# State scan of a delta-rule layer: where one visit of the modulation's products and its transposes stand

## The chip, the cores and the metric

The kernel runs on one core of one Trainium2 chip. The metric is the device time of one execution in microseconds (us). The engines are named as in the profile: PE is TensorE (matmuls), PEld its weight loads, DVE is VectorE, ACT is ScalarE, POOL is GpSimd, SP is SyncE (here the queue that issues the DMAs). The granted clock is the share of TensorE's full speed that the chip allowed.

## The reference, cut to what matters

Two networks run one after the other on 256 tokens of 1024 features. In the first, layers 0 and 3 of four mix their tokens with a delta rule; each head (16 heads of 64) keeps a 64x64 state that is carried over the tokens:

```
def step(state, inp):
    r_t, w_t, k_t, v_t, kk_t, a_t = inp
    sa = jnp.einsum('bhvk,bhk->bhv', state, kk_t)
    state = (state * w_t[:, :, None, :]
             - sa[..., None] * (kk_t * a_t)[:, :, None, :]
             + v_t[..., None] * k_t[:, :, None, :])
    return state, jnp.einsum('bhvk,bhk->bhv', state, r_t)
_, y = lax.scan(step, s0, ...)
```

The second network's two layers are modulated by a vector that depends on the conditions alone, so it can be computed at any earlier time:

```
mx = jnp.split(sc @ w_ada[l] + b_ada[l], N_MOD, axis=-1)
mc = jnp.split(scc @ w_ada[l] + b_ada[l], N_MOD, axis=-1)
```

`w_ada[l]` is a 1024 x 9216 fp32 matrix. Of it the two products have one column each, so what it costs is mostly the reading of the matrix.

## The kernel before, in words

The program is written out by hand for each engine, with semaphores between them; an engine does its instructions in the written order. All matmuls outside the two scans take weights that ACT and POOL split into a high and a low part first.

**The scan** (`pe_scan`, `dve_scan` and the loop over `ch` in `act_rwkv`) runs twice, for layer 0 (from 144.47 us of the profiled execution) and layer 3 (from 1422.81 us). It takes four chunks of 64 tokens (`ch`). In each chunk the recurrence becomes dense algebra on 16 heads, of which half 0 is heads 0 to 7 and half 1 heads 8 to 15 (`HALF`, `halves`):

1. Gram products of the chunk's tokens (lines 1577 and 1582), masked by DVE; for chunks after the first also a product with the carried state (L1611).
2. The right-hand side (L1627), copied by ACT (L1432).
3. The inverse of a triangular 64x64 matrix of each head, by doubling, in levels `lv` 1 to 5. A level has on PE: the first product of half 0 and of half 1 (L1639), each of which ACT copies (L1439); then the second products of half 0 and of half 1 (L1647, and L1650 below level 5), each of which DVE subtracts (L1777, L1780) and masks for the next level (L1746). The first product of a half waits for DVE's work on that half of the level before (`inv_taken`), the second for ACT's copy of that half (`inv_half_taken`).
4. The solution of half 0 and half 1 (L1658), copied by ACT (L1451).
5. Products of outputs and new state that don't need the solution (L1666 and L1669, then L1675), then those that do: outputs L1682 and state L1685, half 0 and half 1, each of which ends with `chunk_out`. ACT copies the outputs (L1454), DVE takes the state (L1807).

**The modulation's products** are put between these. `sp_direct` loads `w_ada` in rounds of four panels of 512 KB each into three sets of buffers; from round 3 on a load waits until the round three before it has been used (`direct_used`). Two rounds of a layer's 18 are used ahead of the scan, four in each chunk. A round is used in two halves (`pe_ada_half`, L1496: four 128x512 matmuls, each of which stands twice in the profile), all in bank 7. In a chunk, `fill()` is called 25 times (`VISITS`); the calls counted in `ADA_VISITS` do one half-round each, eight in all. Visit 0 stands before the right-hand side, visits 4(lv-1)+1 to 4(lv-1)+4 before the four half products of level lv, 21 and 22 before the solution's halves, 23 and 24 before the last products' halves.

After the last half-round of a chunk ACT copies bank 7 to a buffer (`act_ada_rows`, L1511), PE transposes it back (`pe_ada_turn`, L1506, at visit 21) and ACT stores four pieces of it (`act_ada_place`, L1518) as its last work of the chunk. The next chunk's visit 0 waits for that (`ada_ready`), and so does PE after the last chunk.

When the rounds of `w_ada` are issued, SP issues the four first panels of `rw{layer}.out` into the buffers of round 15, as each of those has been used (line 605); ACT converts the first of them after the scan (L633).

Of the kernel before, what the change touches and what calls it, by code (L numbers as in the profile page):

```python
# [221 lines left out]
def build(nc, a, out, CONST_AT):  # L222
# [8 lines left out]
    with ExitStack() as ctx:  # L231
# [766 lines left out]
        def tiles_of(name):  # L998

            return G[name].t0 + G[name].n_tiles  # L1000
# [172 lines left out]
        INV_BANKS = [(bank[0], bank[1], bank[2]), (bank[3], bank[4], bank[6])]  # L1173
        OUT_BANKS, STATE_BANKS = (bank[5], bank[4]), (bank[2], bank[6])
        ADA_BANK = bank[7]
        VISITS = 1 + 5 * 4 + 4
        ADA_VISITS = (0, 3, 6, 9, 12, 15, 18, 20)
        CENTRE = sb("CENTRE", P, at=a_at)
        CENTRED, SPREAD = bank[0:4], bank[4:8]
        FIRST_TILES = 3  # L1180
# [204 lines left out]
        def act_rwkv(act, layer):  # L1385
            j = layer // 3
            parts = lora_parts(layer)
            act_entry(act, layer)
            if layer == 0:
                act_cond(act)  # L1390
            act_lora(act, parts[0], j)
            act_panels(act, f"rw{layer}.k")
            act_lora(act, parts[1], j)
            if layer:
                act_lora(act, parts[2], j)
            act.wait_ge(bank_free, tiles_of(f"rw{layer}.k"))
            act.wait_ge(lora_in, after(act, lora_in, len(parts)))
            for c in range(C):
                cs, scale = slice(c * S, (c + 1) * S), vec("rw_k_k", j, c)
                act.activation(RW_P[:, cs], RW_K[:, cs], ACT.Copy, scale=scale)  # L1400
                op = act.activation(RW_B[:, cs], RW_K[:, cs], ACT.Square, scale=scale)
            op.then_inc(keys_ready, 1)
            tile = act_panels(act, f"rw{layer}.v", by_hand=True)
            tile(0)
            act_lora_mid(act, parts[-1])
            tile(1)
            act.wait_ge(lora_taken, after(act, lora_taken, 8 * len(parts)) - 8)
            for c in range(C):
                cs = slice(c * S, (c + 1) * S)
                op = act.activation(RW_T[:, cs], RW_A[:, cs], ACT.Identity, scale=vec("rw_k_a", j, c), bias=KEPT[:, c:c + 1])  # L1410
            op.then_inc(blend_ready, 1)
            tile(2)
            tile(3)
            act.wait_ge(head_taken, after(act, head_taken))
            act_inverse_root(act, RW_T[:, :])
            act.wait_ge(decay_ready, after(act, decay_ready))
            act.activation(RW_XB[:, :], RW_CUM[:, :], ACT.Exp, scale=DECAY).then_inc(exp_ready, 1)
            act.wait_ge(exp_ready, after(act, exp_ready))
            act.activation(RW_CUM[:, :], RW_CUM[:, :], ACT.Exp, scale=-DECAY).then_inc(exp_ready, 1)
            act.wait_ge(exp_ready, after(act, exp_ready))  # L1420
            for s in range(4, C):
                tile(s)
            act_ada_rows(act, bank[0], ADA_FIRST)
            act_lora_out(act, parts[-1], j)
            act_ada_place(act, layer // 3, bank[0], 0, ADA_FIRST)
            for ch in range(NCH):
                for t, b in ((VT, 1), (BT, 1), (CT, 0)):
                    if ch < NCH - 1 or t is VT:
                        act.wait_ge(turned_ready, after(act, turned_ready))
                        act.activation(t, bank[b][:, :], ACT.Copy).then_inc(turned_taken, 1)  # L1430
                act.wait_ge(rhs_ready, after(act, rhs_ready))
                act.activation(RHS, bank[5][:, :], ACT.Copy).then_inc(rhs_taken, 1)  # L1432
                for lv in range(1, 6):
                    for h, banks in zip(HALF, INV_BANKS):
                        act.wait_ge(inv_half, after(act, inv_half))
                        o, i = IT[:, h], banks[0][:, h]
                        if lv == 5:
                            o, i = blocks(o, lv, 1), blocks(i, lv, 1)
                        act.activation(o, i, ACT.Copy).then_inc(inv_half_taken, 1)  # L1439
                    if ch == 1 and lv < 5:  # L1440
                        if lv == 1:
                            act.wait_ge(bonus_gated, after(act, bonus_gated))
                        for c in (2 * lv - 2, 2 * lv - 1):
                            cs = slice(c * S, (c + 1) * S)
                            op = act.activation(RW_G[:, cs], RW_G[:, cs], ACT.Copy, scale=vec("rw_ln_w", layer // 3, c))
                        if lv == 4:
                            op.then_inc(gate_scaled, 1)
                act_ada_rows(act, ADA_BANK, 4)
                for h, banks in zip(HALF, INV_BANKS):
                    act.wait_ge(sol_ready, after(act, sol_ready))  # L1450
                    act.activation(SOL[:, h], banks[0][:, h], ACT.Copy, scale=-1.0).then_inc(sol_taken, 1)  # L1451
                for k, h in enumerate(HALF):
                    act.wait_ge(chunk_out, after(act, chunk_out))
                    act.activation(v3(RW_Y)[:, k * C // 2:(k + 1) * C // 2, ch * CHUNK:(ch + 1) * CHUNK],  # L1454
                                   OUT_BANKS[k][:, h].rearrange("p (c t) -> p c t", t=CHUNK),
                                   ACT.Copy).then_inc(y_taken if ch < NCH - 1 else head_in, 1)
                act_ada_place(act, layer // 3, ADA_BANK, ADA_FIRST + 4 * ch, 4)
            out_panels = G[f"rw{layer}.out"]
            pairs = [slice(2 * p * S, 2 * (p + 1) * S) for p in range(4)]

            def squared_pair(p):
                act.wait_ge(centred, after(act, centred))
                act.activation(RW_B[:, pairs[p]], CENTRED[p][:, :], ACT.Square).then_inc(centre_squares, 1)

            for slot in range(RING):
                counts.start(act, raw_landed[slot], 16 * out_panels.p0 // RING)
            act_round(act, out_panels, 0)
            act.activation(log_probe[:, :], eps[:, 2:3], ACT.Ln)
            squared_pair(0)
            squared_pair(1)  # L1470
            act_round(act, out_panels, 1)
            squared_pair(2)
            squared_pair(3)
            act_round(act, out_panels, 2)
            for p in range(4):
                act.wait_ge(spread_ready, after(act, spread_ready))
                act.activation(SPREAD[p][:, :], SPREAD[p][:, :], ACT.Ln, bias=eps[:, 2:3], scale=1.0 / DH).then_inc(act_step, 1)
            for p in range(4):
                act.wait_ge(act_step, after(act, act_step))
                act.activation(SPREAD[p][:, :], SPREAD[p][:, :], ACT.Exp, scale=-0.5).then_inc(root_ready, 1)  # L1480
            for p in range(4):
                act.wait_ge(y_gated, after(act, y_gated))
                act.activation(OUTH[:, pairs[p]], SPREAD[p][:, :], ACT.Copy).then_inc(hi_part, 1)
            act_round(act, out_panels, 3)
            act_panels(act, f"rw{layer}.out")
# [51 lines left out]
        def pe_scan(pe, layer):  # L1537
# [14 lines left out]
            def fill():  # L1552

                ch, v = visits[0] // VISITS, visits[0] % VISITS
                visits[0] += 1
                if v in ADA_VISITS:
                    if ch and v == 0:
                        pe.wait_ge(ada_ready, after(pe, ada_ready))
                    n = ADA_VISITS.index(v)
                    pe_ada_half(pe, ADA_FIRST + RING * ch + n // 2, n % 2, ADA_BANK)  # L1560
                elif v == VISITS - 4:
                    pe_ada_turn(pe, ADA_BANK, 4)

            pe.wait_ge(scan_in, after(pe, scan_in))
# [1 line left out]
            for ch in range(NCH):  # L1566
# [110 lines left out]
                for h in range(2):  # L1677
                    fill()
                    pe.wait_ge(side_done, after(pe, side_done))
                    pe.wait_ge(sol_taken, after(pe, sol_taken))  # L1680
                    for c, r in halves[h]:
                        mm = pe.matmul(sq(OUT_BANKS[h], c, r), sq(SOL, c, r), sq(GBQ, c, r), start=False, stop=c in lasts)  # L1682
                    if not last:
                        for c, r in halves[h]:
                            mm = pe.matmul(sq(STATE_BANKS[h], c, r), sq(BT, c, r), sq(SOL, c, r), start=False, stop=c in lasts)  # L1685
                    mm.then_inc(chunk_out, 1)
            assert visits[0] == NCH * VISITS
            pe.wait_ge(ada_ready, after(pe, ada_ready))

# [1799 lines left out]
```

## Time and profile before

| | |
|---|---|
| time, median of 3 runs | 3872.2 us |
| lowest and highest run | 3850.99 and 3883.87 us |
| the profiled execution's own time | 3878.49 us |
| its span, first to last instruction | 3876.7 us |
| granted clock over the span | 0.982 |
| PE busy | 3714.3 us (96%) |
| layer 0's scan, 144.47 to 301.54 us | 157 us |
| layer 3's scan, 1422.81 to 1584.35 us | 162 us |

A row of the timeline begins with the start and the duration in us, then engine, line and operation, output and inputs, shapes, and how many instructions are put together; in brackets stands how long the engine had been idle and what it waited for. "issue" is time in which the engine waited for nothing that the profile shows. A row of waits gives the total, the number of times and the longest. A row of windows gives the stretch, its length, then the busy time and number of instructions of PE, PEld, DVE, ACT and POOL, the granted clock, the DMA share and GB/s.

### The profile page before, as it was taken

Reading aid. Unit: us, or ns where it says so; the run is one execution under the profiler, and the core shown is the slowest. Engines: PE = TensorE matmul, PEld = TensorE weight load, DVE = VectorE, ACT = ScalarE, POOL = GpSimd, SP = SyncE. Lnnn points to the kernel's source line nnn. Section 1 sums busy time; section 2 is a strip of 40 time slices with the busy share of each in tenths; the row PEclk is TensorE's granted clock in tenths of the full one; section 3 lists DMA queues with packets and bytes.
Section 4 is the critical chain, followed back from the end, with each engine's and each line's share of the span. In section 5 each row is a group of like instructions: output and inputs, shape, how many; then the busy total and the mean of one; then the engine's idle time right before and its main releaser. Section 6 shows DMA issues by size and latency. Waiting matters only on the chain.

```text
span 3876.7 us, 93136 instructions
## 1 busy us (share of the span) xinstructions
PE 3714.3 (96%) x35973; PEld 3531.0 (91%) x35973; DVE 1585.0 (41%) x3475; ACT 1880.4 (49%) x2758; POOL 2634.3 (68%) x1186
## 2 busy tenths in 40 slices
PE   8988998999899898899999999999999999999998
PEld 7668997998699766799999999999999999999998
DVE  6533315315632653333222474753123222266442
ACT  5325447444454342545555555465555555555643
POOL 5006873884288500488888878769888888886886
PEclk9999999999999999999999999999999999999999
DMA  6564652674366355466666646556666666664664
GB/s 187 197 215 136 185 172 83 186 199 110 85 181 183 118 171 202 136 195 185 193 187 184 192 142 189 151 146 202 194 191 183 192 178 199 190 188 129 186 179 141
DMA packets 1162953, 664.96 MB, mean 172 GB/s; under 512 B 30157, under 2 KB 1122201, under 8 KB 1162551
## 3 DMA queue, kind: packets, MB, share of 16 engines
q1 hardware_dynamic: 1162679, 661.06, 57.8%
q8 instruction: 202, 3.31, 0.4%
q14 instruction: 72, 0.59, 0.1%
HBM read 659.92 MB, written 1.05 MB: 170 GB/s over the span
## 4 chain that ended last, share of the span: by engine, by line
PE 60%; issue 24%; POOL 10%; DVE 4%; ACT 1%; DMA 0%; POOLq 0%; DVEq 0%; SPq 0%; ACTq 0%
PE bank L863 57%; POOL wlo L623 10%; PE bank L842 1%; DVE bank L3138 1%; ACT whi L633 0%; PE bank L1064 0%; DMA raw<-in_ffn_w_gu 0%; DMA raw<-in_w_in 0%; PE bank L2779 0%; PE bank L2827 0%; PE bank L2845 0%; PE bank L963 0%; DVE W L2063 0%; DVE W L2076 0%; DVE W L2061 0%
## 5 line engine op out<-in xcount | busy, mean ns | idle before, releaser
L623 POOL TENSOR_TENSOR wlo<-raw,whi 128x1024 fp32r<-128x1024 f32 (+3 forms) x1182 | 2634.1, 2245 | 1218.6 <-ACT whi L633 1214.5
L633 ACT ACTIVATE whi<-raw 128x1024 fp32r<-128x1024 f32 (+3 forms) x1182 | 1170.7, 995 | 1088.1 <-PE bank L863 925.4
L863 PE MATMUL bank<-AH,whi 128*128 128x256 f32 (+1 forms) x5712 | 1605.5, 281 | 24.1 <-DVE AL L773 10.1
L863 PE MATMUL bank<-AL,whi 128*128 128x256 f32 x5712 | 1598.2, 280 | 0.0
L863 PE MATMUL bank<-AH,wlo 128*128 128x256 f32 (+1 forms) x5712 | 1597.5, 280 | 0.0
L863 PEld LDWEIGHTS bank<-AH,whi 128*128 128x128 f32 x5712 | 1084.0, 190 | 33.3 <-issue 19.2
L863 PEld LDWEIGHTS bank<-AH,wlo 128*128 128x128 f32 x5712 | 1081.7, 189 | 0.0
L863 PEld LDWEIGHTS bank<-AL,whi 128*128 128x128 f32 x5712 | 1077.8, 189 | 0.6
L863 PE MATMUL bank<-HH,whi 128*128 128x256 f32 x1936 | 541.6, 280 | 0.0
L863 PE MATMUL bank<-HH,wlo 128*128 128x256 f32 x1936 | 539.7, 279 | 0.0
L863 PE MATMUL bank<-HL,whi 128*128 128x256 f32 x1936 | 539.6, 279 | 0.0
L863 PEld LDWEIGHTS bank<-HH,whi 128*128 128x128 f32 x1936 | 366.2, 189 | 0.5
L863 PEld LDWEIGHTS bank<-HH,wlo 128*128 128x128 f32 x1936 | 364.9, 188 | 0.0
L863 PEld LDWEIGHTS bank<-HL,whi 128*128 128x128 f32 x1936 | 363.9, 188 | 0.2
L1082 DVE TENSOR_TENSOR bank<-silu,bank 128x256 f32<-128x256 f32 x132 | 56.6, 429 | 529.5 <-PE bank L863 529.5
L1036 ACT ACT_TABLE_LOAD x60 | 77.0, 1283 | 105.5 <-PE bank L863 105.5
L863 PE MATMUL bank<-OUTH,whi 128*128 128x256 f32 x432 | 121.6, 281 | 3.1 <-issue 2.4
L863 PE MATMUL bank<-OUTL,whi 128*128 128x256 f32 x432 | 120.8, 280 | 0.0
L863 PE MATMUL bank<-OUTH,wlo 128*128 128x256 f32 x432 | 120.8, 280 | 0.0
L1116 DVE TENSOR_TENSOR bank<-bank,RSTD 128x256 f32<-128x256 f32 x110 | 47.3, 430 | 168.2 <-PE bank L863 168.2
L1036 ACT ACTIVATE silu<-bank 128x256 f32<-128x256 f32 x132 | 50.7, 384 | 127.2 <-PE bank L863 126.5
L928 DVE TENSOR_TENSOR X<-X,bank 128x256 f32<-128x256 f32 (+1 forms) x64 | 26.6, 418 | 205.5 <-PE bank L863 194.4
(453 smaller groups left out, 4783.6 us busy)
## 6 DMA issues: line engine op xcount, KB each, us to landing
raw<-in_ffn_w SPq DMA_DIRECT2D x420, 512.0 KB, 4.0
raw<-in_w_in SPq DMA_DIRECT2D x182, 512.0 KB, 3.9
raw<-in_ffn_w_gu SPq DMA_DIRECT2D x176, 512.0 KB, 3.8
ada_raw<-in_w_ada SPq DMA_DIRECT2D x96, 512.0 KB, 6.6
raw<-in_ffn_w_down SPq DMA_DIRECT2D x64, 512.0 KB, 4.0
raw<-in_rw_w_rkv SPq DMA_DIRECT2D x48, 512.0 KB, 4.1
raw<-in_w_ada SPq DMA_DIRECT2D x48, 512.0 KB, 6.2
raw<-in_ffn_w SPq DMA_DIRECT2D x56, 384.0 KB, 3.5
```

What stands on the lines that cost most here:

```text
L623: pool.tensor_tensor(wlo[slot][:, 0:n], raw[slot][:, 0:n], whi[slot][:, 0:n], ALU.subtract).then_inc(lo_ready, 1)
L633: act.activation(whi[slot][:, 0:n], raw[slot][:, 0:n], ACT.Copy).then_inc(hi_ready, 1)
L842: mm = pe.matmul(ps, o, w, start=k == c == n == 0, stop=k == g.pps - 1 and c == nk - 1 and n == 2)
L863: mm = pe.matmul(ps[:, 0:o.shape[2]], w, o[:, k0 + c, :], start=tile not in started and c == n == 0, stop=last_panel and c == nk - 1 and n ...
L928: dve.tensor_tensor(o, o, banks[0][:, 0:S], ALU.add).then_inc(bank_free, 1)
L1036: act.activation(silu[j % 2][:, :], bank[(g.t0 + j * g.tiles) % RING][:, 0:S], ACT.Silu).then_inc(silu_ready, 1)
L1082: dve.tensor_tensor(hidden, silu[j % 2][:, :], banks[1][:, 0:S], ALU.mult).then_inc(bank_free, 2)
L1116: dve.tensor_tensor(up, banks[1][:, 0:S], RSTD[:, :], ALU.mult).then_inc(bank_free, 2)
L3138: op = dve.scalar_tensor_tensor(o, i, w, ps, ALU.mult, ALU.add)
```

## The change

The visits that do a half-round are others, the turn (ACT's copy of bank 7, PE's transposes) comes after the solution, and a 26th visit is added to each chunk for it. Half-rounds before: ahead of the right-hand side (0), level 1 second product of half 0 (3), level 2 first product of half 1 (6), level 3 first of half 0 (9), level 3 second of half 1 (12), level 4 second of half 0 (15), level 5 first of half 1 (18), level 5 second of half 1 (20). After: 0, level 1 second of half 1 (4), level 2 second of half 1 (8), then 12, 15, 18, 20 as before, and the last before the output and state products of half 0 (23). PE's transposes move from visit 21 to visit 25, which stands behind `chunk_out` of half 1. On ACT the copy L1511 moves from ahead of the two copies of the solution to behind them.

```
-        VISITS = 1 + 5 * 4 + 4
-        ADA_VISITS = (0, 3, 6, 9, 12, 15, 18, 20)
+        VISITS = 1 + 5 * 4 + 4 + 1
+        ADA_VISITS = (0, 4, 8, 12, 15, 18, 20, 23)
...
-                act_ada_rows(act, ADA_BANK, 4)
                 for h, banks in zip(HALF, INV_BANKS):
                     act.wait_ge(sol_ready, after(act, sol_ready))
                     act.activation(SOL[:, h], banks[0][:, h], ACT.Copy, scale=-1.0).then_inc(sol_taken, 1)
+                act_ada_rows(act, ADA_BANK, 4)
...
-                elif v == VISITS - 4:
+                elif v == VISITS - 1:
                     pe_ada_turn(pe, ADA_BANK, 4)
...
                     mm.then_inc(chunk_out, 1)
+                fill()
```

## Rows read from the trace of the kernel before

**Rows 1.** The page's first part: busy time, share of the span, instructions.

```profile
PE 3714.3 (96%) x35973; PEld 3531.0 (91%) x35973; DVE 1585.0 (41%) x3475; ACT 1880.4 (49%) x2758; POOL 2634.3 (68%) x1186
```

**Rows 2.** Windows of single chunks: first and last of layer 0, last of layer 3.

```profile
144.47:181.07 36.60, 34.49 (x962) 26.29 (x964) 17.04 (x46) 7.44 (x18) 0.00 (x0) 0.95 0.67 232
...
266.55:301.54 34.99, 32.85 (x908) 24.69 (x905) 13.54 (x38) 7.01 (x21) 0.00 (x0) 0.98 0.40 123
...
1538.90:1584.35 45.45, 39.51 (x910) 28.48 (x906) 13.88 (x39) 7.01 (x21) 0.00 (x0) 0.81 0.35 110
```

**Rows 3.** Waits of PE in layer 0's scan.

```profile
PE bank L1577 <- issue: 5.7, 4, 2.9
PE bank L1675 <- issue: 5.3, 2, 2.7
PE bank L1639 <- DVE scan L1746: 2.0, 4, 0.5
PE bank L1506 <- ACT ada_tok L1511: 1.3, 4, 0.4
...
PE bank L1647 <- ACT scan L1439: 0.2, 1, 0.2
```

**Rows 4.** Waits of PE in layer 3's scan.

```profile
PE bank L1577 <- issue: 7.4, 5, 3.2
PE bank L1675 <- issue: 2.9, 1, 2.9
...
PE bank L1506 <- ACT ada_tok L1511: 0.9, 3, 0.3
```

**Rows 5.** Timeline, chunk 0 of layer 0: starts of levels 2, 3 and 4.

```profile
157.20 0.25 PE L1650 MATMUL bank<-scan,scan 64*64 64x32 f32 x2
157.53 0.68 PE L1639 MATMUL bank<-scan,scan 64*64 64x64 f32 x16
...
162.63 1.15 PE L1639 MATMUL bank<-scan,scan 64*64 64x64 f32 x32
...
167.53 0.42 DVE L1746 TENSOR_TENSOR scan<-W,cst 128x256 f32<-128x256 f32 x1
...
168.00 0.68 PE L1639 MATMUL bank<-scan,scan 64*64 64x64 f32 x16 [0.50 <-DVE scan L1746]
```

**Rows 6.** Timeline, the same chunk: ACT's copies in level 1, and PE's visit 3.

```profile
153.72 0.60 ACT L1432 ACTIVATE scan<-bank 128x512 f32<-128x512 f32 x1 [1.78 <-PE bank L1627]
154.22 0.38 ACT L1439 ACTIVATE scan<-bank 128x256 f32<-128x256 f32 x1
154.38 0.64 PE L1496 MATMUL bank<-ada_raw,cond 128*32 128x512 f32 x4
```

**Rows 7.** Timeline, the same chunk: last visit, ACT's copy, the transposes, the solution's copies.

```profile
174.30 1.06 PE L1496 MATMUL bank<-ada_raw,cond 128*32 128x512 f32 x8
...
175.51 0.60 ACT L1511 ACTIVATE ada_tok<-bank 128x512 f32<-128x512 f32 x1 [1.28 <-PE bank L1496]
...
176.25 0.63 PE L1506 MATMUL bank<-cst,ada_tok 128*128 128x128 f32 x4 [0.30 <-ACT ada_tok L1511]
...
177.53 0.85 ACT L1451 ACTIVATE scan<-bank 128x256 f32<-128x256 f32 x2 [1.43 <-PE bank L1658]
```

**Rows 8.** Timeline, end of layer 0's scan, and the DMAs that SP issues before it.

```profile
301.87 0.38 ACT L1518 ACTIVATE both<-bank 128x8 f32<-128x8 f32 x4
...
302.30 0.48 PE L1730 MATMUL bank<-W,CENTRE 128*128 128x256 f32 x1 [0.76 <-ACT both L1518]
...
283.78 25.69 SPq L562 DMA_DIRECT2D raw<-in_rw_w_out  x6
```

**Rows 9.** Windows: a wait for issue in layer 0's scan, and 3.3 us soon after.

```profile
182.40:185.30 2.90, 0.00 (x0) 0.00 (x0) 1.28 (x2) 0.58 (x1) 0.00 (x0) 1.00 0.18 64
186.00:189.30 3.30, 2.63 (x101) 2.44 (x93) 2.44 (x5) 0.00 (x0) 0.00 (x0) 0.50 0.02 5
```

**Rows 10.** The page's third part: the queue that fetches instructions.

```profile
q8 instruction: 202, 3.31, 0.4%
```

## The prediction, made before the changed kernel was run

> **What bounds the kernel now.** I read the page's first part before anything else: PE is busy for 96% of the span [rows 1], so time is lost or won on PE alone unless a wait is opened on it. The change touches only the eight chunks of the two scans, so I cut these out as windows. A chunk takes 35 to 45 us, and in chunk 0 PE is busy for 34.49 of 36.60 us [rows 2]. The reader is to see that the scan too is bound by PE: there is hardly any waiting time left in a chunk that a visit could still fill. Third, the list of PE's waits in each scan says what the rest is [rows 3, 4]. Two kinds stand there. Waits for other engines are short and the same in each chunk: four waits for DVE in each scan (the row of [rows 3] stands word for word in layer 3's list too), 2.0 us in all, so 0.5 us for each chunk, and about 0.3 us for ACT's copy ahead of the transposes. Waits for "issue" are longer and irregular: the largest groups alone are 5.7, 5.3 and 7.4 us, single ones up to 3.2 us. Last, the timeline of one chunk shows which half product each short wait precedes.
>
> **The work that only moves.** A half-round is 8 records in 1.06 us on PE, the transposes are 4 records in 0.63 us [rows 7]. Both are done as often as before: eight half-rounds and one set of transposes a chunk. PE works in order and is nearly always busy, so the work itself costs the same in any place: 0. What changes is only which waits it covers. The new calls of the fill routine that do nothing issue nothing, and ACT's copy is one either way.
>
> **Waits that open in the inverse.** In the timeline, level 4 already has the pattern that levels 2 and 3 get. A half-round stands ahead of the second product of half 1 of level 3, and none ahead of the first products of level 4. Half 0 of level 4 starts at once (DVE had the length of the half-round for it), and half 1 waits: DVE's mask ends at 167.53 + 0.42 = 167.95 us, PE starts at 168.00 after 0.50 us idle [rows 5]. Level 3 before the change has the half-round ahead of its half 0, and its two first products run through in 1.15 us without a wait [rows 5]; in level 2 the half-round stands between the halves. After the change both levels have the same order as level 4, so each gets its wait: 2 x 0.50 = +1.00 us a chunk. The work of DVE on a half is three instructions of equal shape in levels 1 to 3, so the same 0.50 us holds; bounds are 0.3 and 0.75 us for each, since DVE and ACT also have a few gate instructions in the first two chunks.
>
> In level 1 the half-round moves from ahead of the second product of half 0 to ahead of half 1. There ACT is late: it first copies the right-hand side, then half 0, which ends at 154.22 + 0.38 = 154.60 us. PE could begin the second product at 154.38, where the half-round starts now, and so waits 0.22 us and some 0.05 for the signal, as in the step from 167.95 to 168.00: +0.27 us [rows 5, 6]. Its bounds are 0 and 0.4 us.
>
> **Waits that close.** The transposes wait for ACT's copy: 1.3 us over four chunks and 0.9 over three [rows 3, 4], a good 0.30 us a chunk. After the change ACT has copied bank 7 while PE does the output and state products, some 2 us, so nothing is left: -0.30 us. What is late next is the solution of half 1, which needs DVE's last subtraction; that lies at the end of the solution of half 0, and I give it +0.05 us. Level 2 now starts 0.08 us after PE is free (157.20 + 0.25 = 157.45 to 157.53) [rows 5]; the half-round ahead of half 1 covers this: -0.08. The short waits for ACT's copy, of 0.2 us once in a scan [rows 3], go too.
>
> **Between solution and outputs.** ACT's two copies of the solution end at 177.53 + 0.85 = 178.38 us [rows 7], while PE is busy with products that don't need them; no row shows PE waiting for these copies in any chunk. The half-round put there covers nothing: 0. ACT's copy of bank 7 (0.60 us) now stands ahead of its copies of the outputs; it runs while PE does the output and state products of half 0, twice 16 records of the 0.68 us kind [rows 5], less their overlap, and is hidden except in the last chunk, where it about ends with them.
>
> **At a chunk's end.** PE's transposes stand ahead of the next chunk's Gram products, and need a bank of their own, so nothing else waits for them but ACT's stores (0.38 us, rows 8), which the next chunk's visit 0 awaits; all Gram products of that chunk lie between. In the last chunk PE waits for the stores: 0.76 us idle now [rows 8]. Then the transposes (0.63) run beside the copies of the outputs, and the stores (0.38) come behind them, about 1.03 us from the last output product to the next matmul: +0.3 us in each scan, of which the work itself is counted above.
>
> **Queues.** Some half-rounds come up to three visits later, so SP's loads of the next rounds start later, by at most some 4 us (three visits are less than the 5.4 us from the start of level 3 to that of level 4's second half, rows 5). No row of waits shows PE waiting for a panel inside the scans. The panels of the projection behind the scan, now issued from 283.78 us, are first used by ACT and PE after 302 us [rows 8]; 3 us later still leaves 15 us. Cost 0; if that cover failed it would be a few us, once in a scan. POOL has nothing to do in the scans.
>
> **The sum.** A chunk: +1.00 +0.27 -0.30 +0.05 -0.08 = +0.94 us. Eight chunks: +7.5. Less about 1 us for the short ACT waits and the longer transposes' wait of one chunk, plus 0.6 at the two ends: +7 us. The profiled execution took 3878.49 us and would take 3885.5. It lies 6.3 us over the median of the runs; on the median of 3872.2 the forecast is 3879 us, 0.2% more. A measurement of this kernel tells about 1% (39 us) from no change, and the runs before span 33 us, so I forecast: no change that can be told.
>
> **What may shift more than the sum.** The waits for issue are over 18 us in the three largest groups, more than twice the sum. They stand in the dense stretches: Gram products, and the products behind the solution. The change brings a half-round and the transposes (1.7 us that need few instructions) into that stretch and takes the transposes and their wait from ahead of the solution. Bounds: all of these 18 us gone, or one more wait of the largest kind (3.2 us, rows 4) in each chunk, +26 us. I take 0, the middle of an irregular pattern.
>
> The page Runtime: NRT & Kernel Launch of the Trainium skill, section Instruction fetch mechanics, says that instructions come in 16 KiB blocks, the next fetched while one is executed, and that this is mostly hidden. The block size agrees: 202 packets, 3.31 MB [rows 10]. That it is hidden does not hold in the dense stretches here, if these waits are fetches. By the rule the sum would stay +7 us and nothing else could move it; by the rows it may move by the amounts above.
>
> **Rivals.**
>
> 1. The waits for issue absorb it: a PE that waits for DVE in the inverse gives the fetch time, and what is added there is missing later. For it: the groups of issue waits are larger than the 7 us. Against: the solution lies 14 us behind the start of level 3 (162.63 to 176.88 us, rows 5, 7). Then -5 us: 3867 us.
>
> 2. One more long issue wait in each chunk: 8 x 3.2 = 26 less some that end sooner: +24 on top of +7, 3903 us. For it: such waits come and go between chunks that have the same instructions. Against: total instructions don't change.
>
> 3. Slower by over 1%, by the clock. After the wait of 2.90 us for issue, PE ran at 0.50 of its clock, the lower level of 1.2 GHz, in 186.00 to 189.30 us [rows 9]; and layer 3's last chunk, at a clock of 0.81, took 45.45 us against the 34.99 of its counterpart at 0.98, for the same work [rows 2]. Two more half-microsecond waits, and a stretch from level 1 to level 3 with a half-round less, could bring the clock down in the inverse. If each chunk then lost what the 10.5 us between these two chunks suggest, less 4 us that are issue waits, that is 6.5 x 8 = 52: 3872 + 7 + 52 = 3931 us; it decides from five or six chunks on. Against it: level 4's 0.50 us wait is there in every chunk, and chunks 0 and 3 still have mean clocks of 0.95 and 0.98 [rows 2]. TensorE: Matmul & The Clock Gate in the Trainium skill, section HAM oscillation, tells of a loop in which repeated waits bring the engine back to half rate each time. Its rule speaks for this rival; here only the waits of about 3 us were followed by the lower level.
>
> 4. The issue waits go. If all 18 us of the largest groups went, and with them the 6.5 us that the low clock takes in layer 3's last chunk, it would be 3872 + 7 - 25 = 3854 us. Faster by over 1% needs still more, from the smaller groups and the clock of other chunks. For it: the half-round and the transposes stand right where these waits are. Against: they last 1.7 us together, a long wait 3.
>
> 5. It does not do what it says, that is, the moved loads make PE wait for panels: +3 us in some chunks, 3890 us.
>
> **How the numbers follow.** Forecast 0.60, with a range of its own from 3864 to 3894 (the runs' spread about +7); rival 1 0.22, rival 2 0.08, rival 3 0.04, rival 4 0.04, half of it beyond 1%, rival 5 0.02. Faster 0.02, slower 0.04, the rest, 0.94, within 1%. The range from 3856 to 3903 us leaves out rival 3, most of rival 4 and the tails of the spread.
>
> **What would show it.** In the list of PE's waits, L1639 for DVE should rise from four to about twelve in each scan (2.0 to 6 us), L1506 for ACT should vanish, and L1647 for ACT should have about 0.3 us in each chunk. PE's busy time should not move. The wait ahead of L1730 should be about 0.4 us behind the transposes. Wrong would be: no new waits of L1639; PE waiting at L1682 for the copies of the solution; a granted clock under 0.95 in most chunks; any wait for a DMA in a chunk.

## The result, and the profile after

The changed kernel takes 3893.1 us (median of 17 runs, 3870.89 to 3905.16), the kernel before in the same sessions 3874.91 us (17 runs, 3850.99 to 3883.87). The ratio is 1.0045, with a 95% interval of 1.0032 to 1.0059: 17.4 us slower (12.4 to 22.9). That is within the 1% that was called no change, and within the range, but it is clear of noise, and more than twice the +7 us of the sum. Three executions in the experiments below ran at a far lower granted clock (0.55 to 0.84 over the span) and are left out of the ratios.

The page's first part, changed kernel:

```profile
span 3885.3 us, 93136 instructions
PE 3707.6 (95%) x35973; PEld 3520.5 (91%) x35973; DVE 1586.3 (41%) x3475; ACT 1880.3 (48%) x2758; POOL 2634.9 (68%) x1186
```

As many instructions as before, PE not busier over the whole span [rows 1], the span longer: the added time is not more work. The two scans, up to the first product behind them, took 157.83 and 162.30 us before; now 170.25 and 168.36:

```profile
145.87:316.12 170.25, 144.53 (x3920) 107.66 (x3920) 59.03 (x163) 34.92 (x99) 0.00 (x0) 0.94 0.54 179
1428.92:1597.28 168.36, 144.02 (x3921) 107.91 (x3921) 59.02 (x163) 34.93 (x99) 0.00 (x0) 0.95 0.53 178
```

In these two windows together PE is idle 12.8 us longer than before (50.1 against 37.3 us), and 5.7 us longer busy (288.6 against 282.9); the second profile of each kernel gives 12.8 and 9.0 us. Where a product no longer overlaps the next one, or the clock is lower, the same products are busy for longer.

The waits of PE in the first of these, which answer to [rows 3]:

```profile
PE bank L1577 <- issue: 11.1, 5, 3.7
PE bank L1639 <- DVE scan L1747: 6.3, 12, 0.9
PE bank L1682 <- issue: 3.3, 2, 1.9
PE bank L1675 <- issue: 2.7, 1, 2.7
PE bank L1611 <- issue: 0.9, 1, 0.9
PE bank L1647 <- ACT scan L1439: 0.6, 3, 0.2
```

and in the second, which answer to [rows 4]:

```profile
PE bank L1577 <- issue: 8.6, 5, 2.8
PE bank L1639 <- DVE scan L1747: 5.9, 12, 0.5
PE bank L1675 <- issue: 3.5, 1, 3.5
PE bank L1496 <- issue: 2.2, 1, 2.2
PE bank L1682 <- issue: 1.9, 1, 1.9
PE bank L1627 <- issue: 0.8, 1, 0.8
```

Two things are to be seen. The waits of L1639 for DVE are twelve in each scan instead of four, and the wait of L1506 for ACT has gone, both as forecast. But all rows that end in "issue" together are 18.0 + 17.0 = 35.0 us; in the two lists of the kernel before they are 13.2 + 14.8 = 28.0 us. That is 7 us of the step to which the prediction gave 0.

The start of level 2 in chunk 0, half 1 with no half-round before it, answers to the row at 168.00 us of [rows 5]:

```profile
160.45 0.42 DVE L1747 TENSOR_TENSOR scan<-W,cst 128x256 f32<-128x256 f32 x1
...
160.92 0.68 PE L1639 MATMUL bank<-scan,scan 64*64 64x64 f32 x16 [0.49 <-DVE scan L1747]
```

**A table of fixed parts.** Since a chunk is always the same work, I took from the timeline the distance from one start to the next, in stretches without a wait for issue and at full clock. There it repeats within about 0.02 us from chunk to chunk and from profile to profile. A few places have a second value in some chunks, 4.92 beside 4.85 us in level 4, 4.30 beside 4.37 in level 1; that this comes from the gate instructions of DVE and ACT is likely, not shown. In us:

| stretch of a chunk | before | after | turn_only | drop20 | last22 | v14 |
|---|---|---|---|---|---|---|
| level 1 | 4.23 | 4.37 | 4.23 | 4.23 | 4.37 | 4.23 |
| level 2 | 5.10 | 4.69 | 5.10 | 5.10 | 4.69 | 5.10 |
| level 3 | 4.19 | 4.69 | 4.19 | 4.19 | 4.69 | 4.19 |
| level 4 | 4.85 | 4.85 | 4.85 | 4.85 | 4.85 | 4.16 |
| level 5, turn before the solution | 5.14 | 4.12 | 4.12 | 3.25 | 4.12 | 5.14 |
| solution half 0 to L1666 | 0.76 | 0.92 | 0.92 | 0.77 | 1.88 | 0.76 |
| L1675 to L1682 | 0.71 | 2.03 | 0.71 | 2.03 | 0.71 | 0.71 |
| L1682 of half 1 to the next chunk | 0.83 | 1.62 | 1.62 | 1.62 | 1.62 | 0.83 |

After against before the table gives +0.14 -0.41 +0.50 -1.02 +0.16 +1.32 +0.79 = +1.48 us in each of six chunks; in the last chunk of a scan the end grows by 0.59 instead of 0.79, and the wait behind it falls from 0.76 us [rows 8] to 0.47, so +0.99. Together 6 x 1.48 + 2 x 0.99 = 10.9 us. The stretch from a chunk's first Gram product to level 1 is not in the table, because issue waits fall into it; in chunk 0 of layer 3, less its issue waits, it is 6.20 us in both profiles of both kernels.

### The profile page after: what moved, and what is told of

It is laid out like the page before. It is cut to its first block, busy times and chain, and to the rows that moved or that the text cites. A ratio compares the mean times of both kernels' runs of the same rounds, so it can differ in the third digit from the quotient of the medians.

```text
span 3885.3 us, 93136 instructions
## 1 busy us (share of the span) xinstructions
PE 3707.6 (95%) x35973; PEld 3520.5 (91%) x35973; DVE 1586.3 (41%) x3475; ACT 1880.3 (48%) x2758; POOL 2634.9 (68%) x1186
## 4 chain that ended last, share of the span: by engine, by line
PE 59%; issue 25%; POOL 11%; DVE 4%; ACT 1%; DMA 0%; POOLq 0%; DVEq 0%; SPq 0%; ACTq 0%
PE bank L863 56%; POOL wlo L623 11%; PE bank L842 1%; DVE bank L3139 1%; ACT whi L633 0%; PE bank L1064 0%; DMA raw<-in_w_in 0%; PE bank L2828 0%; PE bank L2780 0%; PE bank L2846 0%; PE bank L963 0%; DVE W L2064 0%; DVE W L2077 0%; DVE W L2062 0%; POOLq L622 0%
```

## The experiments

The time of each is a ratio to the kernel before, run beside it on the same chip. "Issue waits" are the rows of the list of PE's waits that end in "issue", added up over both scans: one profile for each kernel, unless said. The expectations count 29 us of them for the kernel before and 33.5 for the changed one; the lists add up to 28.0 and 35.0, and these are used here.

**turn_only: the transposes and ACT's copy alone.**

```
-        VISITS = 1 + 5 * 4 + 4
+        VISITS = 1 + 5 * 4 + 4 + 1
...
-                act_ada_rows(act, ADA_BANK, 4)
                 for h, banks in zip(HALF, INV_BANKS):
...
+                act_ada_rows(act, ADA_BANK, 4)
...
-                elif v == VISITS - 4:
+                elif v == VISITS - 1:
...
+                fill()
```

> The transposes and ACT's copy of bank 7 move behind the solution and the last products as in the change; the half-rounds stay at the visits of the kernel before. Theory A (the extra time is waits for DVE and ACT that levels 1 to 3 got, plus 64x64 products that no longer overlap where the moved work stands): per chunk, level 5 with the turn behind it falls from 5.14 to 4.1 us, the solution's first half rises from 0.76 to 0.92, the stretch from the last products to the next chunk rises from 0.83 to 1.62, in sum -0.1 us a chunk; levels 1 to 3 stay 4.23, 5.10, 4.19 us. Time against before: -1 us, 0.998 to 1.002. Theory B (the extra time comes from more issue waits, because work moved into the dense stretch at a chunk's end): issue waits rise as in the changed kernel, about half of its 17 us: 1.002.

Ratio 0.9984 (0.9966 to 1.0002). The fixed parts came out as expected (table): the turn gives 1.02 us ahead of the solution, and takes 0.79 at the chunk's end and 0.16 in the solution, where DVE's last subtraction is now late. Issue waits 12.1 + 12.8 = 24.9 us, not more than before: work moved behind the last products does not by itself bring issue waits. Theory B, in the form that it had, fell here.

**turn_only_again: the same kernel.**

> The kernel with the turn alone moved, timed once more beside the one before it in this call: fixed parts as in its first profile (-0.1 us a chunk against before), ratio 0.9984 the first time, of which 0.1% at most is fixed by the program. If issue waits come out near 26 us again and lower clock near 14 us (29 and 34 us before), its gain is in these; if not, it was the spread.

Ratio 0.9994 (0.9970 to 1.0018), issue waits 13.3 + 13.2 = 26.5 us, granted clock in the scans 0.96 and 0.98 where the first profile had 0.97 and 0.99. The issue waits are the same within 2 us; that this part makes the kernel faster is not shown.

**drop20: the half-round between solution and outputs is that of visit 20.**

```
-        ADA_VISITS = (0, 4, 8, 12, 15, 18, 20, 23)
+        ADA_VISITS = (0, 3, 6, 9, 12, 15, 18, 23)
```

> The changed kernel, but the half-round that goes to between solution and outputs is that of visit 20 (level 5, second product of half 1), and the others stay where they were before. Theory A: levels 1 to 3 are as before (4.23, 5.10, 4.19 us), nothing opens in level 5 but about 0.1 us; left are 1.3 us for the half-round between solution and outputs against the 1.05 that it took in level 5, and the turn's -0.1: +0.3 us a chunk, +2 to +3 us in all, 1.0007 (1.000 to 1.002). Waits of L1639 for DVE: four in each scan, not twelve. Theory B: as slow as the changed kernel, 1.0045, since the dense stretch is the same as there.

Ratio 1.0023 (1.0005 to 1.0040). No wait opens in the inverse; four waits for DVE, as before:

```profile
PE bank L1577 <- issue: 11.3, 5, 4.7
PE bank L1639 <- DVE scan L1747: 2.0, 4, 0.5
PE bank L1650 <- issue: 1.6, 1, 1.6
```

Level 5 without visit 20 and the turn falls by 1.89 us, and L1675 to L1682 rises by 1.32 for the half-round that is put there. The fixed parts together are +0.23 us a chunk, under 2 us in all; issue waits are 14.4 + 15.8 = 30.2 us, 2.2 more than before. The time is slightly above what was expected (1.000 to 1.002), and about half of the changed kernel's, though the two intervals overlap. The fixed parts say more clearly than the time that it matters which half-round is taken out of the inverse: +0.23 us a chunk here, +1.48 in the changed kernel. So the early levels' waits are a real part of the 17 us.

This profile also has the longest issue waits of all, 5.0 and 4.7 us. They are taken up again under late_loads.

**last22: the last half-round between the halves of the solution.**

```
-        ADA_VISITS = (0, 4, 8, 12, 15, 18, 20, 23)
+        ADA_VISITS = (0, 4, 8, 12, 15, 18, 20, 22)
```

> The changed kernel, but its last half-round stands between the two halves of the solution (visit 22) and not ahead of the output products. Theory A: it costs about 1.07 us there, not 1.32, and covers the 0.15 us that half 1 of the solution waits for DVE: -0.4 us a chunk against the changed kernel, so +14 us against before, 1.0036. The levels 1 to 3 as in the changed kernel. Theory B has no number for it, but would let it be as slow as the changed kernel, 1.0045.

The table bears out the step: the same half-round adds 1.88 - 0.92 = 0.96 us at visit 22, where it also covers the 0.16 us by which the solution is late, and 2.03 - 0.71 = 1.32 at visit 23. Issue waits fell too, to 15.3 + 14.8 = 30.1 us. The ratio is 1.0046 (1.0030 to 1.0062), not below the changed kernel's: the 3 us that the fixed parts gain (and 5 of issue waits) don't show in six runs whose interval is 12 us wide. It holds the 1.0036 that was expected as well as the 1.0045 of the changed kernel, so this run decides nothing between them, and no faster kernel came of it.

**v14: the kernel before, one half-round one visit earlier, where PE waits 0.50 us in each chunk.**

```
-        ADA_VISITS = (0, 3, 6, 9, 12, 15, 18, 20)
+        ADA_VISITS = (0, 3, 6, 9, 12, 14, 18, 20)
```

> The kernel before with one half-round moved by one visit, from 15 to 14: it stands between the first products of level 4's halves, where PE waits 0.50 us for DVE in each chunk. Theory A: the waits of L1639 for DVE go (2.0 to 0 us a scan), about 0.1 us opens at the start of level 5; -0.4 to -0.5 us a chunk, -3 to -4 us in all, 0.999. Theory B: no change of the time that one can tell, issue waits take back what the DVE waits gave.

Level 4 falls from 4.85 to 4.16 us: a wait shown as 0.50 us costs 0.69, since the products on both sides of it also lose their overlap. Nothing opens in level 5. Eight times 0.69 is 5.5 us, a ratio of 0.9986; measured is 0.9997 (0.9977 to 1.0017), which neither shows that gain nor excludes it. In this profile layer 0's scan had a granted clock of 0.90:

```profile
144.48:312.15 167.67, 148.22 (x3921) 111.66 (x3921) 59.05 (x163) 34.56 (x99) 0.00 (x0) 0.90 0.53 182
```

Its issue waits were 17.0 + 13.4 = 30.4 us. So in this profile what the fixed parts gave was given back there.

**turn_v14: both together.**

> The two parts that paid for themselves together: the turn behind the last products as in the change, half-rounds at the visits of the kernel before but for 15, which goes to 14. What is fixed by the program: level 4 4.16 us instead of 4.85, level 5 4.1 instead of 5.14, solution 0.92, chunk's end 1.62: -0.75 us a chunk against before, -6 us, 0.9985. Issue waits and clock can hide or double this: 0.996 to 1.001.

The fixed parts are as expected (4.16, 4.12, 0.92, 1.62), the ratio is 1.0013 (0.9987 to 1.0039). Issue waits 28.4 us, the clock 0.93 and 0.96. No version that beats the kernel before came out of this.

**before_again and after_again: each kernel profiled once more.**

> The kernel before, profiled once more. If the parts of a chunk without a wait for issue and at full clock are fixed by the program, levels 1 to 3 are 4.23, 5.10 and 4.19 us again, level 5 with the turn 5.14, and all that differs from the first profile (29 us of issue waits in the two scans, 34 us at the lower clock) stands in the issue waits and the clock. By how much they differ is what one profile can't tell: I expect up to 4 us of issue waits and 10 us of lower clock either way.

> The changed kernel, profiled once more: levels 1 to 3 again 4.37, 4.69, 4.69 us, the half-round behind the products without the solution again 2.03 us with them. Theory A: issue waits in the scans, 33.5 us the first time, may come out near the 29 us of the kernel before. Theory B: they are above those of the kernel before again, by 3 us or more.

The fixed parts are the same to 0.02 us. Issue waits: 13.9 + 14.1 = 28.0 us for the kernel before (28.0 the first time), 19.6 + 15.9 = 35.5 for the changed one (35.0). So they are not scatter but belong to the kernel: +7.2 us. The scatter is in the clock: the scans of the kernel before had 0.96 and 0.94 in the first profile and 0.96 and 0.97 in the second, those of the changed one 0.94 and 0.95, then 0.95 and 0.95. The two scans together took 320.1 and 316.2 us before, 338.6 and 338.1 after: 20.2 us apart in the mean, of which the fixed parts are 10.9, the issue waits 7.2, and 2 are left, for the clock (lower by 0.01 in the mean) and for whatever overlap the issue waits themselves cost.

Outside the two scans both kernels have the same work. It took 3556.6 and 3528.1 us in the profiles of the kernel before, 3546.7 and 3559.7 in those of the changed one. Single profiles are therefore compared by the scans only, never by the span.

**before_half_loads and after_half_loads: half the bytes of the modulation's matrix in the scans.** Both leave out half of each panel's sum there.

```
+                    if rnd >= ADA_FIRST:
+                        sp.dma_start(dst[:, 0:ADA_N], src[0:P, :]).then_inc(landed, 16)
+                        continue
                     sp.dma_start(dst[:, :].rearrange("p (c m) -> p c m", m=ADA_N),
...
-                data[:, half * ADA_N:(half + 1) * ADA_N],
+                data[:, :ADA_N] if rnd >= ADA_FIRST else data[:, half * ADA_N:(half + 1) * ADA_N],
```

> The kernel before with half the bytes of each panel of w_ada loaded in the scans' 16 rounds (256 KB of 512), and the first half of a panel used twice: this leaves out half of the modulation's columns' sums there. If the fetch of PE's instructions is held up by this traffic, the issue waits (29 us) fall to some 20 us, time 0.997 of before. If they are a matter of the instruction stream alone they stay at 26 to 32 us, ratio 1.000.

> The changed kernel with the same halved loads (half of each panel's sums left out in the scans). Theory A: against the kernel before with the same edit it is slower by the same 0.3 to 0.45%, as what is fixed by the program (11 us) has nothing to do with loads. If the loads, which start up to 4 us later after the change, had a part in it, the distance between the two shrinks to under 0.2%.

Before with half loads: ratio 0.9939 (0.9919 to 0.9958). Every engine's work in the scans is what it was; the two scans' windows:

```profile
145.63:293.68 148.05, 134.34 (x3921) 101.29 (x3921) 58.89 (x163) 34.63 (x99) 0.00 (x0) 1.00 0.35 110
1392.77:1540.94 148.17, 134.29 (x3920) 101.32 (x3920) 58.88 (x163) 34.62 (x99) 0.00 (x0) 1.00 0.36 110
```

The two together are 296.2 us, against 320.1 and 316.2. Issue waits fell from 28.0 to 9.0 + 9.2 = 18.2 us, the longest from 3.2 to 1.8 us, and the lower clock was gone too, which the expectation of 0.997 had left out. After with half loads: 0.9961 (0.9943 to 0.9980), issue waits 8.3 + 10.5 = 18.8 us. The distance between the two kernels is 0.9961/0.9939 = 1.0022, or 8.5 us, near the 10.9 us of the fixed parts. The two intervals leave this distance uncertain by about 0.0027, so the time alone does not choose between the two theories. The profiles say more: the scans are 13.5 us apart (309.7 against 296.2), and the 7 us of issue waits have shrunk to 0.6. What is fixed by the program stays. The changed kernel's order of PE's work is there with half loads too, so it is not this order by itself that brings the added issue waits; the loads have a part in them.

**late_loads: the kernel before, only the time of the loads moved.** In both kernels the loads of a round start when an earlier round has been used up. The change has the half-rounds that use one up at visits 4, 12, 18 and 23, not 3, 9, 15 and 20, so more of the traffic falls into the dense stretch from the solution to the next right-hand side. The first of these stretches in the kernel before, then in the changed one:

```profile
176.81:192.21 15.40, 11.79 (x457) 10.56 (x457) 6.50 (x12) 3.30 (x11) 0.00 (x0) 0.89 0.41 148
```

```profile
178.09:199.37 21.28, 15.63 (x474) 12.54 (x471) 7.08 (x14) 4.20 (x12) 0.00 (x0) 0.84 0.52 188
```

The last column is GB/s: 15.40 us at 148 are 2.3 MB, 21.28 us at 188 are 4.0 MB. Over the six stretches the loads alone are 13.3 MB against 23.8. To move nothing but this, SP alone is made to wait:

```
                     sp.wait_ge(panels_done, before)
+                if rnd in (7, 11, 15):
+                    sp.wait_ge(sol_ready, 8 * int(name[3:]) + (rnd - 7) // 2 + 1)
                 for j in range(RING):
```

> The kernel before; the engines' programs are as they were, only SP holds the loads that it issues in chunks 0 to 2 of a scan after visit 15 until the first half of the solution is done, so that they and those behind them run into the last products and the next chunk's Gram products, as the loads of the changed kernel do. Theory C (the changed kernel's issue waits, 35 us in two profiles against 28, come from more load traffic in the dense stretches between solution and next right-hand side: 23.8 MB there against 13.3): issue waits in the two scans rise to 32 us or more, the parts of a chunk without them stay at 4.23, 5.10, 4.19, 4.85, 5.14 us, time 1.001 to 1.003 of before. Theory D (they come from where the visit and the transposes stand in PE's own instruction stream): issue waits stay at 26 to 30 us, time 1.000.

Ratio 1.0070 (1.0044 to 1.0096), 27 us, more than theory C expected. The six stretches now move 25.2 MB. The waits in layer 0's scan (lines are two further down than in the kernel before; each engine but SP has its old program):

```profile
PE bank L1579 <- issue: 15.6, 5, 3.6
PE bank L1613 <- issue: 4.2, 1, 4.2
PE bank L1641 <- DVE scan L1748: 2.0, 4, 0.5
PE bank L1508 <- ACT ada_tok L1513: 1.2, 4, 0.3
```

Issue waits are 20.7 + 20.2 = 40.9 us against 28.0; the waits for DVE and ACT and all fixed parts are those of the kernel before. Theory D falls. The two scans are 338.7 us, about as long as the changed kernel's; the issue waits are 12.9 us of the growth, and the clock is lower too (0.93 and 0.92, before 0.94 to 0.97). What the window of one such wait shows is DMA engines that are full while PE stands:

```profile
182.00:185.00 3.00, 0.06 (x5) 0.04 (x4) 1.29 (x2) 0.60 (x1) 0.00 (x0) 1.00 1.05 397
```

The packets of the instruction queue ([rows 10], 16 KB each) say how. Behind every issue wait of over 1 us in the scans of all thirteen profiles, PE goes on 2.2 to 2.9 us after such a packet starts, with much traffic or none. What moves is its start. For these waits it lies between 1.6 us before PE has run out and 0.65 us after in the kernel before (0.9 in its second profile), with half loads never after, in the changed kernel up to 1.3 us after, in late_loads always after, up to 1.8 us. The wait of 5.0 us in drop20 can be cut in two at the start of the packet: in the 2.46 us ahead of it the DMA engines are busy for 0.87 of the time and move 322 GB/s, in the 2.50 us behind it for 0.17, at 57 GB/s. So the traffic does not make the fetch itself slower, it makes it start later.

The bytes in the dense stretches do not give the issue waits by themselves. drop20 has 17.3 MB there and 30.2 us, late_loads 25.2 MB and 40.9 us, but last22 has 23.2 MB, nearly as much as the changed kernel, and only 30.1 us instead of 35. That it counts whether a packet falls due while loads are running would fit, but it is not shown, and no run here explains the difference between last22 and the changed kernel.

## Why the prediction was right, and where it was not

**What bounds the kernel** held: PE, with no room left in a chunk. So did the forecast that nothing is gained, and the band of within 1%.

**Waits that open in the inverse** held to the row: twelve waits for DVE in each scan, 6.3 and 5.9 us, about 0.50 each and one of 0.9; ACT's 0.2 us in level 1, in three of four chunks (+0.27 forecast, +0.14 in the start distances, which count the overlap too). **Waits that close** held: L1506 no longer waits. For the solution's half 1 I gave +0.05, it was +0.16. **Scan's end** held: 0.47 us behind the transposes, 0.4 forecast.

**The work that only moves** was wrong: "costs the same in any place: 0". Before the change, L1675 and L1682 overlap; the first product of L1682 starts 0.71 us after the first of L1675, though the latter's 32 records need 1.10 us where nothing follows closely. Both are 64x64 products, and the records of the two lines alternate:

```profile
178.55 0.93 PE L1675 MATMUL bank<-CTX,W 64*64 64x64 f32 x26
179.26 0.28 PE L1682 MATMUL bank<-CTX,scan 64*64 64x64 f32 x2
179.31 0.28 PE L1675 MATMUL bank<-CTX,W 64*64 64x64 f32 x3
```

In the changed kernel they stand apart:

```profile
180.00 1.10 PE L1675 MATMUL bank<-CTX,W 64*64 64x64 f32 x32
181.03 1.07 PE L1496 MATMUL bank<-ada_raw,cond 128*32 128x512 f32 x8
182.02 0.45 PE L1682 MATMUL bank<-CTX,scan 64*64 64x64 f32 x8
```

The half-round costs 1.32 us in this place, against 0.96 at visit 22 and 4.12 - 3.25 = 0.87 at visit 20; the transposes, 0.63 us in their row [rows 7], cost 0.79 at the chunk's end. So +1.48 us a chunk came out, not +0.94. Of the 0.54 between them, 0.26 are the half-round (1.32 for 1.06), 0.16 the transposes, 0.11 the solution, and 0.10 levels 1 to 3, where waits also cost overlap; 0.09 go off again ahead of the solution. Over the kernel that is 10.9 us, not 7. The sum was right in its direction, and this term, put at 0, was mis-sized.

**The issue waits** got 0, with bounds of -18 and +26. They were +7.2 us, in both profiles. What failed is the step on queues, which asked of the later loads only whether PE would wait for a panel. It does not, in the scans of any profile. It also put the delay of the loads at "at most some 4 us"; in chunk 0 of layer 0 the four rounds start 2.0, 4.1, 4.6 and 5.3 us later, counted from the chunk's start. But the loads share the DMA engines with the instruction queue, and late_loads shows that the time at which they run can alone cost 0.7%. The chapter Trainium Kernel Development and Optimization of the Trainium skill, section Key Constraints, says that the DMAs issued by different engines run on the same 16 DMA engines and interleave; it speaks of queues that engines issue from. The runs here show that the instruction queue suffers too. The rule that the fetch is mostly hidden (Runtime: NRT & Kernel Launch of the Trainium skill, section Instruction fetch mechanics) does not hold in these scans, where with full loads 25 to 41 us of 308 to 339 are such waits.

**Rivals.** Rival 1, that issue waits absorb the new ones, and rival 4, that they go, had the wrong sign. Rival 2 had the right mechanism in part, without its cause: not one more long wait a chunk, but a third of that. Rival 3: the clock in the inverse did not fall from the 0.50 us waits, of which there are twelve now; levels 2 and 3 took 4.69 us in all chunks of both profiles, but for level 3 of layer 0's chunk 2 (5.05), and the granted clock was below 0.95 in three of the eight chunks, in two of eight before. Its sentence that only the waits of about 3 us were followed by the lower level was a misreading of the kernel before. Its longest stretch at that level stands behind an issue wait of 1.2 us, and PE is busy all through it. The row of the wait in layer 3's scan, then the window of the stretch:

```profile
PE bank L1650 <- issue: 1.2, 1, 1.2
```

```profile
1571.80:1582.00 10.20, 10.20 (x120) 6.35 (x118) 1.29 (x5) 1.79 (x5) 0.00 (x0) 0.50 0.01 4
```

Rival 5 had the right object, the moved loads, and the wrong victim. Fixed parts 10.9 and issue waits 7.2 are 18.1 us, the measured difference is 17.4 (12.4 to 22.9). That the forecast held in spite of a sum that was too small by more than half rests on its width: no change that can be told, and a range of 47 us.

Open is the clock. Without long issue waits (half loads of the kernel before) it never fell in a scan; v14 and turn_v14, which only take short waits away, had low clocks in layer 0's scan (0.90, the lowest of all, and 0.93) and lost in them what they had gained. In v14 two stretches of 10.2 us at 0.50 (from 213.70 and 299.00 us) have no issue wait of over 0.4 us in the 14 us ahead of them. One profile each does not say whether that belongs to the place of the half-round. Open is also whether last22 is faster than the changed kernel, and why its issue waits are fewer.

## What to carry to other kernels

When buffers are freed later, ask not only whether the loads still land in time but what else uses the DMA engines while they run: here that was the queue that fetches PE's instructions. Work used as filler is cheapest where its engine waits anyway, and costs more than its own length between small products that overlap each other; measure a place by the distance from start to start, not by the busy time of the piece. A filler does not need to be moved to where the chain looks long, if PE has no idle time there.

## What the runs showed of the hardware

The same instructions of PE took 13 us more of issue waits when 25.2 MB instead of 13.3 MB were loaded in six dense stretches (late_loads; 119.0 us in all, before 93.9), and 10 us less when the loads were halved. From the start of an instruction packet of 16 KB it took 2.2 to 2.9 us until PE went on, with 0 to nearly 400 GB/s of other traffic beside it.

At a longest issue wait of 1.8 us the clock was 1.00 through both scans (half loads, kernel before). In layer 0's scan of the changed kernel with half loads it was 1.00 beside twelve waits for DVE of 0.5 to 0.9 us; in layer 3's, with two issue waits of 2.1 and 2.2 us, 0.98. But the stretches of about 10 us at the lower level (1571.8 us of the kernel before, two in v14) show that long waits are not the only thing that it falls behind.
